# Rotary halves of the queries exchanged by transfers instead of a matmul, in a fused decoder step on one core

## The reference, cut to what matters

```python
cq = rms_norm(h @ w_dq, q_gain)                      # (520 tokens, 256)
q  = einsum('bsr,rhd->bshd', cq, w_uq)               # 16 heads of 128 + 64 columns
q  = concat([q[..., :128], rope(q[..., 128:], pos)]) # rope on the last 64 columns
q  = rms_norm(q, qk_gain_q) * qk_gain_k
q_lat = einsum('bshn,chn->bshc', q[..., :128], w_uk)

def rope(x, pos):                                    # half = 32
    x1, x2 = x[..., :half], x[..., half:]
    return concat([x1 * cos - x2 * sin, x1 * sin + x2 * cos])
```

## Time and profile before

| | us |
|---|---|
| median of 3 runs | 2081.05 |
| lowest and highest | 2073.68, 2082.86 |
| the profiled execution, its own time | 2079.41 |
| its span | 2077.7 |
| PE busy | 2058.9 (99%) |
| DVE busy | 1601.1 (77%) |
| ACT busy | 1103.1 (53%) |
| POOL busy | 341.7 (16%) |

### The profile page before, as it was taken

One profiled execution on the slowest core, in us unless ns is written; L12 is line 12 of the kernel. 1 busy time (PEld: TensorE's weight loads), 2 busy tenths in 40 slices (PEclk: granted clock), 3 DMA queues, 4 the chain that ended last, 5 costly groups with the idle time before them and its releaser, 6 DMA issues.

```text
span 2077.7 us, 44241 instructions
## 1 busy us (share of the span) xinstructions
PE 2058.9 (99%) x16692; PEld 1993.7 (96%) x16692; DVE 1601.1 (77%) x2667; ACT 1103.1 (53%) x1898; POOL 341.7 (16%) x384
## 2 busy tenths in 40 slices
PE   9999999999999999999999999999999999999999
PEld 8999999999999999999999999998768789999998
DVE  6779885437367998988899898678665468989987
ACT  5446554443225655645665665445564346655555
POOL 0011111221011111111211111111122121111111
PEclk9999999999999999999999999999999999999999
DMA  5467783322224777775777777441322127777775
GB/s 162 121 160 179 187 200 105 91 92 80 84 81 114 176 180 179 180 182 151 172 179 181 187 183 172 138 134 29 96 72 82 61 62 158 178 189 171 198 175 129
DMA packets 362555, 293.57 MB, mean 141 GB/s; under 512 B 21591, under 2 KB 329092, under 8 KB 362148
## 3 DMA queue, kind: packets, MB, share of 16 engines
q1 hardware_dynamic: 326266, 226.84, 36.4%
q0 software_dynamic: 35824, 64.37, 19.1%
q10 hardware_dynamic: 314, 0.37, 0.1%
HBM read 224.57 MB, written 2.66 MB: 109 GB/s over the span
## 4 chain that ended last, share of the span: by engine, by line
PE 85%; DMA 8%; DVE 4%; issue 2%; ACT 1%; SPq 1%; ACTq 0%; DVEq 0%
PE side L825 26%; PE main L776 26%; PE main L825 19%; DMA raw<-raw 3%; DMA sums_w<-raw 2%; PE side L1370 2%; DMA raw<-in_ffn_w_gate 2%; PE main L1130 2%; PE main L1300 1%; DVE w_lo L2104 1%; DMA raw<-in_ffn_w_up 1%; PE side L1340 1%; PE side L1220 1%; PE main L1200 1%; PE side L1044 1%
## 5 line engine op out<-in xcount | busy, mean ns | idle before, releaser
L825 PE MATMUL side<-xw_hi,w_hi 128*128 128x260 f32 x1344 | 381.1, 284 | 5.1 <-ACT main L1545 1.5
L825 PE MATMUL side<-xw_hi,w_lo 128*128 128x260 f32 x1344 | 381.0, 283 | 0.0
L825 PE MATMUL side<-xw_lo,w_hi 128*128 128x260 f32 x1344 | 380.1, 283 | 0.0
L2104 DVE TENSOR_TENSOR w_lo<-raw,w_hi 128x512 fp32r<-128x512 f32 (+2 forms) x472 | 323.4, 685 | 35.5 <-ACT w_hi L1490 16.6
L825 PE MATMUL main<-xw_hi,w_hi 128*128 128x260 f32 x1008 | 286.1, 284 | 0.0
L825 PE MATMUL main<-xw_lo,w_hi 128*128 128x260 f32 x1008 | 284.7, 282 | 0.0
L825 PE MATMUL main<-xw_hi,w_lo 128*128 128x260 f32 x1008 | 284.5, 282 | 0.0
L825 PEld LDWEIGHTS side<-xw_hi,w_hi 128*128 128x128 f32 x1344 | 253.2, 188 | 8.5 <-ACT main L1545 3.0
L825 PEld LDWEIGHTS side<-xw_hi,w_lo 128*128 128x128 f32 x1344 | 253.2, 188 | 0.0
L825 PEld LDWEIGHTS side<-xw_lo,w_hi 128*128 128x128 f32 x1344 | 252.8, 188 | 0.0
L2104 DVE TENSOR_TENSOR w_lo<-sums_w,w_hi 128x1024 fp32r<-128x1024 f32 (+1 forms) x232 | 218.6, 942 | 1.0 <-ACT w_hi L1473 1.0
(11 more groups left out here) (460 smaller groups left out, 5340.8 us busy)
## 6 DMA issues: line engine op xcount, KB each, us to landing
sums_w<-raw POOLq DMA_DIRECT2D x112, 256.0 KB, 3.3
raw<-raw POOLq DMA_DIRECT2D x112, 256.0 KB, 5.1
raw<-in_ffn_w_gate SPq DMA_DIRECT2D x86, 256.0 KB, 4.4
raw<-in_ffn_w_gate SPq DMA_DIRECT2D x43, 512.0 KB, 5.9
raw<-in_ffn_w_up SPq DMA_DIRECT2D x84, 256.0 KB, 4.5
raw<-in_ffn_w_up SPq DMA_DIRECT2D x42, 512.0 KB, 6.2
raw<-in_gmlp_w_in SPq DMA_DIRECT2D x16, 1024.0 KB, 5.3
raw<-in_ffn_w_down SPq DMA_DIRECT2D x56, 256.0 KB, 4.1
```

The source lines that it names most:

```text
L825: mm = nc.tensor.matmul(into[j], w_tiles(w, weights_at(s, j))[:, k, :], moving[:, k, order[j], :], start=(j in (0, 1) and k == 0 and i == ...
L2104: a = nc.vector.tensor_tensor(dst, src, hi.bitcast(F32), ALU.subtract)
```

## The change

`turn_rope` and its eight calls go. A new SBUF tile tq_swapped takes the exchanged halves, and SP issues four transfers of 32 partitions by 520 words for each rotary tile (`swap_halves`), from tq. rope_b is made from tq_swapped, in SBUF. The copy of the rotary tile out of PSUM goes from DVE to ACT, with a semaphore tq_copied. evac_done counts the 16 plain tiles alone.

SP's order: `load_pages(0, 4)` in place of (0, 6) ahead of chunk 2; the exchanges of pairs 0 and 1 ahead of chunk 3; the exchanges of pairs 2 to 7 behind chunk 3, with one `load_pages` step behind that of pair 2 and one behind that of pair 3; then the pages as before. Each exchange from pair 1 on waits until the rope_b before it has read tq_swapped.

DVE's order: rope_b of a pair goes from the first tile of the next pair to its last tile, its sum one tile later; the thirds of the next w_lo are made one ahead of the copy at part 3, one behind the products at parts 3 and 4, instead of ahead of the copies at parts 3, 4 and 5. rope_b and the sum of the last pair stand behind the copies of the key rows.

```diff
+            def swap_halves(r_):
+                sp.wait_ge(tq_copied, r_ + 1)
+                if r_ >= 1:
+                    sp.wait_ge(rope_b_set, r_ + 1)
+                for lo in range(0, P, ROPE // 2):
+                    other = lo ^ ROPE // 2
+                    sp.dma_start(tq_swapped[lo:lo + ROPE // 2, :], tq[other:other + ROPE // 2, r_ % 2, :])\
+                        .then_inc(swapped, 16)
...
             for c in range(4):
                 if c == 2:
                     sp.wait_ge(pages_in, 16)
                     sp.wait_ge(tile_done, at_mla.tile)
-                    load_pages(0, 6)
+                    load_pages(0, 4)
+                elif c == 3:
+                    swap_halves(0)
+                    swap_halves(1)
                 sp.wait_ge(lo_done, at_uq.lo + c - 1)
...
+            for r_ in range(2, H // 2):
+                swap_halves(r_)
+                if r_ in (2, 3):
+                    load_pages(r_ + 2, r_ + 3)
             sp.wait_ge(tile_done, at_wo.tile)
             sp.wait_ge(lo_done, at_wo.lo)
             load_pages(6, 10)
...
-            def turn_rope(u):
-                r_ = u // 3
-                pe.wait_ge(rope_b_set, r_ + 1)
-                pe.wait_ge(evac_done, e + u + 1)
-                wide_sum(0, swap, [tq[:, r_ % 2, :]]).then_inc(swapped, 1)
...
-                pe.wait_ge(evac_done, e + u - 1)
+                if u < 2:
+                    pe.wait_ge(evac_done, e + u - 1)
+                elif u % 3 == 1:
+                    pe.wait_ge(tq_copied, u // 3)
+                else:
+                    pe.wait_ge(evac_done, e + nope_tiles(u - 2))
...
                 mm.then_inc(tile_done, 1)
-                if u % 3 == 0 and u > 0:
-                    turn_rope(u - 1)
                 if u >= 2:
                     q_norms(u - 2)
-            turn_rope(23)
...
-                act.wait_ge(evac_done, e + u + 1)
-                src = tq[:, u // 3 % 2, :] if part % 3 == 2 else qn[:, 4 * c + 2 * (part // 3) + part % 3, :]
+                if part % 3 == 2:
+                    src = tq[:, u // 3 % 2, :]
+                    if u >= 6:
+                        act.wait_ge(tq_squared, u - 5)
+                        act.wait_ge(rope_a_set, u // 3 - 1)
+                        act.wait_ge(swapped, 64 * (u // 3 - 1))
+                    act.wait_ge(tile_done, t + u + 1)
+                    nc.scalar.activation(halves(src), main[:, u % 2, :, 0:HALF], ACT.Copy).then_inc(tq_copied, 1)
+                    act.wait_ge(tq_copied, u // 3 + 1)
+                else:
+                    act.wait_ge(evac_done, e + nope_tiles(u))
+                    src = qn[:, 4 * c + 2 * (part // 3) + part % 3, :]
...
-                nc.vector.tensor_tensor(halves(rope_b[:, :]), side[:, 0:2, 0:HALF], halves(trig_g[:, 1, :]),
-                                        ALU.mult).then_inc(rope_b_set, 1)
+                nc.vector.tensor_tensor(rope_b[:], tq_swapped[:], trig_g[:, 1, :], ALU.mult).then_inc(rope_b_set, 1)
...
-                if u >= 3 and u % 3 == 0:
-                    rope_b_part(u // 3 - 1)
-                if u >= 5 and u % 3 == 2:
-                    rope_sum(u // 3 - 1)
+                if u >= 5 and u % 3 == 2:
+                    rope_b_part(u // 3 - 1)
+                if u >= 6 and u % 3 == 0:
+                    rope_sum(u // 3 - 2)
+                if part == 3:
+                    weights_rest(1)
+                elif part == 4:
+                    weights_rest(2)
                 k_parts(u)
-            rope_b_part(7)
+            rope_sum(6)
...
+            rope_b_part(7)
             rope_sum(7)
```

More of the change, by code:

```diff
@@ L274, in program @@
         tq = cq
+        tq_swapped = sb("tq_swapped", [P, TOK], F32, proj)
         rope_a = sb("rope_a", [P, TOK], F32, proj)
@@ L479, in program, with nope_tiles @@
         at_uq = at_mla.past(chunk=2, tile=4, evac=4, h=2, rms=3)
-        at_wo = at_uq.past(chunk=4, tile=24, evac=24)
+        at_wo = at_uq.past(chunk=4, tile=24, evac=H)
         at_ffn[3] = at_wo.past(chunk=8, tile=16, evac=16, h=H, norm=1, sums=KD, xg=KD, xh=KD)
         at_ffn[3].groups = LAST_GROUPS
+        def nope_tiles(u):
+            return 2 * (u // 3) + min(u % 3, 1) + 1
         P_AT = [0, 1, 3, 6]
@@ L1915, in _ @@
             act.wait_ge(evac_done, e + 3)
-            nc.scalar.activation(square[:, 0, :], c_t[:], ACT.Square).then_inc(c_squared, 1)
+            nc.scalar.activation(square[:, 0, :], c_t[:], ACT.Square).then_inc(cq_squared, 1)
             act.wait_ge(rms_mm, at_mla.rms + 3)
@@ L2785, in _, with weights_rest @@
                 c, part = u // 6, u % 6
-                if part >= 3 and c < 3:
-                    dve.wait_ge(hi_done, at_uq.lo + c + 2)
-                    at = slice((part - 3) * THIRD, (part - 2) * THIRD)
-                    s = (n + c + 1) % 2
-                    a = nc.vector.tensor_tensor(w_lo[:, s, at], raw[:, s, at], w_hi[:, s, at].bitcast(F32), ALU.subtract)
-                    if part == 5:
-                        a.then_inc(lo_done, 1)
-                elif part >= 3:
-                    dve.wait_ge(kv_hi_set, part - 2)
-                    at = kv_third(part - 3)
-                    nc.vector.tensor_tensor(w_lo[:, 0, at], wkv_flat[:, at], kv_hi[:, at].bitcast(F32),
-                                            ALU.subtract).then_inc(kv_lo_set, 1)
-                if part % 3 == 2 and u >= 6:
-                    dve.wait_ge(tq_squared, u - 5)
-                    dve.wait_ge(rope_a_set, u // 3 - 1)
-                dve.wait_ge(tile_done, t + u + 1)
-                dst = tq[:, u // 3 % 2, :] if part % 3 == 2 else qn[:, 4 * c + 2 * (part // 3) + part % 3, :]
-                nc.vector.tensor_copy(halves(dst), main[:, u % 2, :, 0:HALF]).then_inc(evac_done, 1)
+                def weights_rest(i):
+                    if c < 3:
+                        dve.wait_ge(hi_done, at_uq.lo + c + 2)
+                        at = slice(i * THIRD, (i + 1) * THIRD)
+                        s = (n + c + 1) % 2
+                        a = nc.vector.tensor_tensor(w_lo[:, s, at], raw[:, s, at], w_hi[:, s, at].bitcast(F32), ALU.subtract)
+                        if i == 2:
+                            a.then_inc(lo_done, 1)
+                    else:
+                        dve.wait_ge(kv_hi_set, i + 1)
+                        at = kv_third(i)
+                        nc.vector.tensor_tensor(w_lo[:, 0, at], wkv_flat[:, at], kv_hi[:, at].bitcast(F32),
+                                                ALU.subtract).then_inc(kv_lo_set, 1)
+                if part == 3:
+                    weights_rest(0)
+                if part % 3 < 2:
+                    dve.wait_ge(tile_done, t + u + 1)
+                    nc.vector.tensor_copy(halves(qn[:, 4 * c + 2 * (part // 3) + part % 3, :]),
+                                          main[:, u % 2, :, 0:HALF]).then_inc(evac_done, 1)
                 if part % 3 > 0:
```

12 lines of the change are left out of this document (7 added, 5 removed).

## The result

The changed kernel took 2081.88 us (median of 21 runs, 2078.35 to 2086.98), the kernel before 2079.04 (21 runs, 2073.68 to 2084.46). The ratio is 1.0018, with a 95% interval of 1.001 to 1.0025: 0.2% slower, where 0.2% faster was forecast. The profiled execution took 2085.33 with a span of 2083.6; PE was busy for 2053.6 us of it, 5.3 less than before.

A forecast was written before the change was run, and what follows sets the result against it. PE was taken to bound the kernel, with DVE at 88% in the loop. Profiled 2079.4 - 6.0 (exchanges) - 0.9 (loop's end) + 2.1 (page wait) = 2074.6, against the median 2076.2; forecast 2076 us, range 2069 to 2084.

The forecast's parts named there:

- rival 4: In the loop, what PE gains is waited away on ACT's copies, so the time doesn't move: 2081; chance 0.07.
- 6.0 less: In the query loop, seven exchanges of 0.88 us leave PE, 6.16 less, of which about 0.2 is given back at the start.
- I price both at nothing: In the loop, DVE's lost copies and ACT's eight added copies were taken to cost PE no time.
- the cover of 0.9: In the loop, slack of 0.9 us on ACT before PE asks for the rotary tile's copy.
- rival 3: DVE or ACT late in the loop by 0.6 us, four times, 2.4 in all: 2078.6; chance 0.13.
- The end of the loop: From the last tile to the new keys: 2.5 us instead of 3.44, so the new keys begin 6.9 earlier.
- The exchange by transfer: Four issues take 1.65 us, the landing 1.9; 4.4 from rope_b to rope_b, under the 6.1 of a pair.
- rival 2: The exchange's round trip bounds the loop, from a landing of about 4.3 us on: 4.8 slower, 2085.9; chance 0.12.
- The pages: Behind the loop, the first late page comes 3.8 us after the last tile; PE waits 2.1 at y = 9.
- Rival 1: The late pages don't bind at y = 9 and all 6.9 us of the gain stay: 2074; chance 0.18.

The follow-up runs named there:

- e3: The changed kernel with ACT's last third of w_hi at part 2 ahead of the rotary tile's copy and square; ratio to the kernel before 1.0008.
- e4: The changed kernel with POOL's cosine product made over 8 of its 520 columns; ratio to the kernel before 1.0015.
- e1: The changed kernel with the last pair's exchange issued from ACT's queue instead of SP's; ratio to the kernel before 0.9991.
- e2: The kernel before with four spare transfers, into a tile nobody reads, ahead of the late pages in SP's queue; ratio to the kernel before 1.0018.
- e6: The changed kernel with the edits of e1 and e3 together; 2075.14 us, ratio to the kernel before 0.9981.
- e7: The changed kernel with eight matmuls on constants on PE ahead of its wait for the last page at y = 9; ratio to the kernel before 1.002.
- e8: The changed kernel with DVE's thirds of w_lo ahead of the copies, as in the kernel before; ratio to the kernel before 1.0015.
- e10: The changed kernel with four matmuls on constants on PE ahead of its wait for the last page at y = 9; ratio to the kernel before 1.0003.
- e9: e6 with the sum of rope_a and rope_b one tile later; ratio to the kernel before 0.9985.
- e11: The kernel before without the exchange: no permutation matmuls, no transfer, rope_b made from tq itself; ratio to the kernel before 1.0004.

## Why the prediction was wrong

The forecast's sum said 4.8 faster, the trace says 1.7 slower where the scores begin. The 6.5 between them are 2.9 (the loop), 1.1 (the first page), 0.9 (the pages' pace) and 1.5 (the clock), with 0.1 of rounding. In the medians it is 2.8 slower: part of the rest is what is lost behind the scores. The measured 2081.88 lies near rival 4's 2081, but by chance: PE waited for none of ACT's copies in the loop.

**The loop, "6.0 less": it was 3.1.** The step that failed was "I price both at nothing". For ACT the cover of 0.9 was worked out for PE, which asks for the copy of the rotary tile, and for that it held. The third of w_hi behind the square, and DVE's w_lo behind that, were counted once, at the start (0.2). They come at part 3 of each of the three chunks: 3.5 us of DVE's idle time, where before it was 0.7, and 2.2 of the loop (e3). For POOL's product the text had the right mechanism and sized it in rival 3, then let it hide behind 0.9 us of slack for PE. In the changed kernel that slack is gone, and e4 shows 1.0 on PE's path. It was DVE's lateness by ACT's order that had used it up: in e3, without that, sq_lo is as slow and PE's idle time is only 0.3 above that of before (1.19 against 0.92). Here the Trainium skill (SBUF — State Buffer, Who interferes with whom) was right, and the runs agree: sq_lo 0.69 alone and 1.20 to 1.81 beside POOL. The exchange itself was priced a little high: in e3's loop PE is busy for 5.5 less, 0.78 for each of the seven, and not 0.88, which is 0.5 of the 2.9. It seems that the chain's share had in it what the next matmul pays as well; no run shows this.

**The end of the loop, 2.5 from the tile to the new keys:** measured 1440.58 - 1438.05 = 2.53. The copy took 0.58 (0.69 forecast). PE waited for sq_lo, though, and only 0.34.

**The exchange by transfer.** The landing was right: 2.0 against 1.9; rope_b waited once in the changed kernel, for 0.16, and rival 2 (a bound by the round trip) didn't come. The issue was wrong: 0.60 each with the gap where 0.41 was taken. The bounds were 0.34 and 0.51, both of other kinds of transfer, and the value was taken near the lower one.

**The pages.** That they would bind at y = 9 was forecast and is the main finding of e1, e2 and e6. The term was 2.1; it became 5.0, the clock's 1.5 among it. The first page came 4.9 after the tile instead of 3.8 (0.8 by the issues, 0.25 by rope_b, 0.1 by the rest). The 40 pages took 44.52 instead of 43.59. This last 0.9 lies within the scatter of single executions: e7, e8 and e10, with the same queue, took 44.30, 43.56 and 43.71, the kernels built on the one before 43.78 to 44.49, and e9 45.80. That the profile shows 1.7 slower, and not 0.7 as in e8, is chance.

**The clock** stood nowhere in the prediction. A wait was priced as its length. Behind 3.50 us of waiting came 1.5 more, which e10 takes away with PE busy. The Trainium skill (TensorE: Matmul & The Clock Gate, Part 1) says that an idle array falls to 1.2 GHz; the trace agrees, with 0.60 granted over the 4 us behind the wait.

**The rivals.** Rival 1 (pages don't bind) fell. Rival 3 (late four times by 0.6, the loop 2.4 worse) was the nearest: four sq_lo of 1.20 are there, and the loop was 2.9 worse; it came together with the forecast's wait for pages, not in its place. A rival was missing that adds the faults up: each was covered by the same slack, which could be spent once.

## What to carry to other kernels

Work moved to an engine is priced by everything behind it on that engine, and by who waits for that, once for each time it recurs; a slack serves one of two late steps, not both. A small transfer set ahead of a gapless row of transfers moves all of them by its issue time, which may be used 45 us later; another engine's queue can take it. Where PE will wait for microseconds, count the slower clock behind the wait.

## What the runs showed of the hardware

- An issue of 32 partitions by 2080 bytes within SBUF takes SP 0.51 to 0.60 us, more than a page of 104 KB (0.34). ACT's queue takes as long: 2.53 for four.
- The wait's length alone doesn't tell whether the clock falls. At y = 9 it fell behind 3.50, 3.16, 2.82 and 2.57, not behind 1.74 and 0.63; but at the end of e9's loop it fell behind 1.59, with a wait of 0.37 for sq_hi 2 us ahead.
- POOL's product and a DVE product with both inputs in SBUF delay each other by up to 1.2 us (e11: w_lo 1.94 against 0.78, with POOL's at 1.30 meanwhile; rows 11: POOL's 1.96, with w_lo at 0.78): in these rows the one that starts second pays.
